# Gate and up by seven block products, and the down product moved between the phases of the next part

## The reference

```python
x = _layer_norm(ALPHA * x + (1 + g1) * mix_out) * ln1_g[l] + ln1_b[l]
h = _layer_norm(x) * (1 + sc2) + sh2
a = silu(einsum('bsd,df->bsf', h, w_gate[l])) * einsum('bsd,df->bsf', h, w_up[l])
ffn = einsum('bsf,fd->bsd', a, w_down[l])
x = _layer_norm(ALPHA * x + (1 + g2) * ffn) * ln2_g[l] + ln2_b[l]
```

## Time and profile before

| | us |
|---|---|
| median of 3 runs | 3360.29 (3359.33 to 3364.14) |
| the profiled execution, its own time | 3362.47 |
| its span, first to last instruction | 3360.4 |
| TensorE busy | 3103.6 |
| VectorE, ScalarE, GpSimd busy | 1487.3, 1029.2, 1120.6 |
| HBM over the span | 90 GB/s |

### The profile page before, as it was taken

One profiled execution on the slowest core, in us unless ns is written; L12 is line 12 of the kernel. 1 busy time (PEld: TensorE's weight loads), 2 busy tenths in 40 slices (PEclk: granted clock), 3 DMA queues, 4 the chain that ended last, 5 costly groups with the idle time before them and its releaser, 6 DMA issues.

```text
span 3360.4 us, 39114 instructions
## 1 busy us (share of the span) xinstructions
PE 3103.6 (92%) x15050; PEld 2592.3 (77%) x15050; DVE 1487.3 (44%) x2194; ACT 1029.2 (31%) x1602; POOL 1120.6 (33%) x649
## 2 busy tenths in 40 slices
PE   8798997899999979997799999979999998999995
PEld 1587886566666646786799999879999987999994
DVE  2343342888888845687221221452112254221225
ACT  1111111777777755123212112221211122112111
POOL 0122231011111125465333333553333364333333
PEclk9899998999999998998899999989999998999997
DMA  9222324321212106354511112131111213111111
GB/s 351 98 72 83 104 81 125 89 63 51 74 57 63 51 23 206 107 176 155 176 63 63 62 62 100 51 125 66 62 66 68 100 51 126 62 62 62 62 63 50
DMA packets 163881, 305.30 MB, mean 91 GB/s; under 512 B 12846, under 2 KB 100015, under 8 KB 161970
## 3 DMA queue, kind: packets, MB, share of 16 engines
q1 hardware_dynamic: 163766, 303.79, 27.3%
HBM read 237.37 MB, written 66.37 MB: 90 GB/s over the span
## 4 chain that ended last, share of the span: by engine, by line
PE 45%; POOL 3%; issue 2%; DVE 1%; DMA 1%; POOLq 1%; ACT 1%; DVEq 0%; SPq 0%; ACTq 0%
PE ffn_gu L1797 10%; PE ffn_gu L1799 10%; PE ffn_gu L1798 10%; PE ffn_dn L1813 5%; PE ffn_dn L1814 5%; PE ffn_dn L1815 5%; POOL ffn_out L1730 1%; POOL ffn_w_lo L1719 1%; POOLq L1725 1%; DMA ffn_h_in<-scr_h_d 1%; POOL ffn_h_lo L1770 0%; DVE ffn_out L1840 0%; POOL ffn_a_lo L1748 0%; POOL ffn_mv L1724 0%; ACT ffn_h_hi L1675 0%
## 5 line engine op out<-in xcount | busy, mean ns | idle before, releaser
L1797 PE MATMUL ffn_gu<-ffn_h_hi,ffn_w_hi 128*128 128x384 f32 x2112 | 707.6, 335 | 30.6 <-DVE ffn_h_lo L1844 26.0
L1799 PE MATMUL ffn_gu<-ffn_h_hi,ffn_w_lo 128*128 128x384 f32 x2112 | 707.2, 335 | 0.0
L1798 PE MATMUL ffn_gu<-ffn_h_lo,ffn_w_hi 128*128 128x384 f32 x2112 | 707.0, 335 | 0.0
L1719 POOL TENSOR_TENSOR ffn_w_lo<-ffn_w_raw,ffn_w_hi 128x2048 fp32r<-128x2048 f32 x99 | 460.9, 4657 | 407.5 <-ACT ffn_w_hi L1667 406.4
L1859 DVE TENSOR_TENSOR ffn_a_raw<-ffn_sil,ffn_gu 128x384 f32<-128x384 f32 x132 | 73.1, 554 | 945.0 <-PE ffn_gu L1799 944.0
L1797 PEld LDWEIGHTS ffn_gu<-ffn_h_hi,ffn_w_hi 128*128 128x128 f32 x2112 | 397.5, 188 | 32.8 <-issue 26.3
L1798 PEld LDWEIGHTS ffn_gu<-ffn_h_lo,ffn_w_hi 128*128 128x128 f32 x2112 | 397.5, 188 | 1.3
L1799 PEld LDWEIGHTS ffn_gu<-ffn_h_hi,ffn_w_lo 128*128 128x128 f32 x2112 | 397.4, 188 | 0.0
L1813 PE MATMUL ffn_dn<-ffn_w_hi,ffn_a_hi 128*128 128x512 f32 x792 | 315.6, 399 | 46.3 <-DVE ffn_total L1869 17.0
L1871 DVE TENSOR_TENSOR ffn_total<-ffn_total,ffn_dn 128x512 f32<-128x512 f32 x360 | 246.0, 687 | 229.8 <-PE ffn_dn L1815 229.8
L943 DVE TENSOR_REDUCE att_peak<-att_sc 128x1 f32<-128x1024 f32 x256 | 312.6, 1221 | 74.7 <-PE att_sc L761 69.9
(11 more groups left out here) (218 smaller groups left out, 4533.6 us busy)
## 6 DMA issues: line engine op xcount, KB each, us to landing
ffn_w_raw<-in_w_gu SPq DMA_DIRECT2D x132, 512.0 KB, 4.5
ffn_w_raw<-in_w_dn SPq DMA_DIRECT2D x66, 512.0 KB, 4.5
mod_wa<-in_w_ada SPq DMA_DIRECT2D x32, 768.0 KB, 6.7
att_q_t<-scr_qs_d SPq DMA_DIRECT2D x128, 128.0 KB, 2.8
proj_x_in<-in_x SPq DMA_DIRECT2D x18, 512.0 KB, 3.9
tail_x_in<-in_x SPq DMA_DIRECT2D x18, 512.0 KB, 3.4
scr_x_d<-tail_w_raw SPq DMA_DIRECT2D x18, 512.0 KB, 5.4
scr_h_d<-tail_direct SPq DMA_DIRECT2D x18, 512.0 KB, 6.1
```

Source lines behind the costliest of these rows:

```text
L1719: nc.gpsimd.tensor_tensor(w_lo[:, i, :], w_raw[:, i, :], w_hi[:, i, :].bitcast(F32), ALU.subtract).then_inc(wlo_done[i], 1)
L1797: nc.tensor.matmul(dst, w_hi[:, i, cols], h_hi[:, k, tokens], start=(k == 0), stop=False)
L1798: nc.tensor.matmul(dst, w_hi[:, i, cols], h_lo[:, k, tokens], start=False, stop=False)
L1799: m = nc.tensor.matmul(dst, w_lo[:, i, cols], h_hi[:, k, tokens], start=False, stop=(k == KD - 1))
```

## The change

Gate and up are each one product of a 1024 x 256 weight block with 1024 x 768 activations, and each of these is cut into 2 x 2 blocks and computed by the Strassen-Winograd scheme: seven block products of 4 steps (half of the width), in place of eight. For this:

- `fourier_and_mix` writes seven operands per pair of tiles to `h7_d` in place of `h2_d`: three blocks of `h2` and four sums of blocks (`operands` on VectorE, behind the tile's own work). `x1_n` is computed by ScalarE with a bias from GpSimd. The 1 of 1 + g is added where the modulation rows are made.
- A part of `ffn` is two phases, gate (`F = 2 * G`) and up (`F + 1`), each with seven weight operands of 128 x 512, three of them sums that VectorE makes (`sums_w`, `last_sum_w`). The raw weights have one buffer for both phases, and operand j of a phase takes the place of operand j of the phase before. ScalarE and GpSimd split each operand.
- VectorE and ScalarE read each product out of one of 4 banks into `sil` or `up`; most products are added to one or two of the four result blocks (`take`).
- The down product of part G-1 stands between the gate and the up phase of part G; the last part's stands behind its own up phase. Down weights have one raw buffer of half a part. The second half of part G-1's is split in the gate phase of part G, the first half of part G's in its up phase.
- A block's input is 21 chunks of 128 x 512, loaded through 4 slots, two of three split by GpSimd and one by VectorE.
- The sample tiles come first (`FFN_ORDER`), so each block has one gate row but for the end of the last. Output tiles are normalised in `total`; in the last block GpSimd does the shift of four tiles.

The core of the diff, with its new functions (added loops and declarations of the same kind are left out):

```diff
@@ fourier_and_mix
+            def operands(t):
+                b11, b21, b12, b22 = h2[:, 0, 0:4, :], h2[:, 0, 4:, :], h2[:, 1, 0:4, :], h2[:, 1, 4:, :]
+                nc.vector.tensor_tensor(t1, b12, b11, ALU.subtract)
+                nc.vector.tensor_tensor(t3, b22, b12, ALU.subtract)
+                dve.drain()
+                nc.vector.tensor_tensor(t2, b22, t1, ALU.subtract)
+                dve.drain()
+                nc.vector.tensor_tensor(t4, b21, t2, ALU.subtract).then_inc(tsum_done, 1)
-                    normalise(1, before, x1_n[:], x1[:, before, :]).then_inc(n2_done, 1)
+                    nc.scalar.activation(x1_n[:], x1[:, (t - 1) % 2, :], ACT.Identity, bias=mv[:, 1, (t - 1) % 2, 5:6],
+                                         scale=mv[:, 1, (t - 1) % 2, 3:4]).then_inc(n2_done, 1)
@@ ffn, SyncE
-                    for i in range(3):
-                        sp.wait_ge(wlo_done[i], G + 1)
-                        weights(0 if is_part(part, PARTS - 1) else part + 1, i)
+            def weights(part, which, F):
+                if begun(F):
+                    sp.wait_ge(wlo_done, OPERANDS * F)
...
+            def down_weights(part, i, G):
+                if i or begun(G):
+                    sp.wait_ge(dnlo_done, 2 * G + i)
...
+                weights(part, 1, F + 1)
+                down_weights(part - 1, 1, G - 1)
...
+                down_weights(part, 0, G)
+                if closes(part):
...
+                    down_weights(part, 1, G)
+                    if not is_last(b, part):
+                        for c in range(CHUNKS7):
+                            hidden(b + 1, c // PAIRS, c % PAIRS)
+                        weights(0, 1, F + 3)
...
+                else:
+                    weights(part + 1, 0, F + 2)
@@ ffn, ScalarE, a step (refill(j) is split_w(F + 2, j) and, in the closing part, split_h(b + 1, j))
+                copy_first(F, sil[:, 0, 0, :])
+                if not is_part(part, 0):
+                    split_down(G - 1, 1)
...
+                for j in (0, 1):
+                    split_w(F + 1, j)
+                silu(G, 1, 1)
+                split_w(F + 1, 2)
+                silu(G, 0, 0)
...
+                copy_first(F + 1, up[:, 0, 0, :])
+                if not is_part(part, 0):
+                    split_down(G, 0)
+                refill(0)
+                if closes(part):
+                    split_down(G, 1)
+                refill(1)
+                split_a(G, 0)
+                refill(2)
+                split_a(G, 1)
+                split_a(G, 2)
+                refill(3)
+                split_a(G, 3)
+                refill(4)
+                refill(5)
+                refill(6)
@@ ffn, GpSimd, a step: split_w(F + 1, 0 to 6), then the same order from refill(0) on
@@ ffn, TensorE
+            def phase(b, part, F):
+                for j in range(OPERANDS):
+                    pe.wait_ge(wlo_done, OPERANDS * F + j + 1)
...
+                    for k in range(4):
+                        cols = slice(k * P, (k + 1) * P)
+                        nc.tensor.matmul(dst, w_hi[:, j, cols], h_hi[:, j, k, :], start=(k == 0), stop=False)
+                        nc.tensor.matmul(dst, w_hi[:, j, cols], h_lo[:, j, k, :], start=False, stop=False)
+                        m = nc.tensor.matmul(dst, w_lo[:, j, cols], h_hi[:, j, k, :], start=False, stop=(k == 3))
+                    m.then_inc(prod_done, 1)
+            def down(G):
+                pe.wait_ge(dnlo_done, 2 * G + 2)
+                for m_ in range(BANKS):
...
+                    if m_ >= 4 or begun(G):
+                        pe.wait_ge(added, BANKS * G + m_ - 3)
...
+            def step(b, part, G):
+                phase(b, part, 2 * G)
+                if not is_part(part, 0):
+                    down(G - 1)
+                phase(b, part, 2 * G + 1)
+                if closes(part):
+                    down(G)
@@ ffn, VectorE
+            def sums_w(F):
+                dve.wait_ge(raw_landed, 32 * (F + 1))
+                nc.vector.tensor_tensor(both[:], raw[:, 1, 0, :], raw[:, 1, 1, :], ALU.add)
+                dve.drain()
+                nc.vector.tensor_tensor(raw[:, 1, 0, :], raw[:, 0, 0, :], raw[:, 1, 0, :], ALU.subtract)
+                nc.vector.tensor_tensor(less[:], both[:], raw[:, 0, 0, :], ALU.subtract).then_inc(wsum_done, 1)
+            def last_sum_w(F):
+                dve.wait_ge(wlo_done, OPERANDS * F + 2)
+                nc.vector.tensor_tensor(less[:], raw[:, 0, 1, :], less[:], ALU.subtract).then_inc(wsum_done, 1)
+            def take(F, j, first, dst):
+                dve.wait_ge(prod_done, OPERANDS * F + j + 1)
+                return nc.vector.tensor_tensor(dst, first, gu[:, j % 4, 0:HALF], ALU.add)
...
+                first_takes(F, sil, in_gate)
+                if opens:
+                    last_sum_w(F + 1)
+                else:
+                    split_down(G - 1, 1)
+                    sums_w(F + 1)
...
+                last_take(F, sil, 4)
...
+                last_take(F, sil, 5)
+                last_take(F, sil, 6)
...
+                if not opens:
+                    last_sum_w(F + 1)
+                    down(b, part - 1 if isinstance(part, int) else part, G - 1)
+                    if not is_last(b, part):
+                        sums_w(F + 2)
+                first_takes(F + 1, up, in_up)
...
+                multiply(G, 0)
...
+                last_take(F + 1, up, 4)
+                multiply(G, 1)
```

More of the change, by code:

```diff
@@ L1497, in _ @@
             combine(1)
-            for t in range(NT + 1):
+            for t in range(NT + 3):
                 slot, before = t % 2, 1 - t % 2
+                if t >= 4 and t % 2 == 0:
+                    operands(t - 4)
                 if t < NT:
@@ L1576, in ffn @@
+        y_stored = [s.sem(f"y_stored{i}") for i in range(TILES)]
         block = ctx.enter_context(nc.Block())
@@ L1581, in parts @@
                 step(b, 0, PARTS * b)
-                with eng.Fori(1, PARTS - 1) as part:
+                step(b, 1, PARTS * b + 1)
+                with eng.Fori(2, PARTS - 1) as part:
                     step(b, part, PARTS * b + part)
@@ L1647, in step @@
[L1647 to L1656 removed]
+                F = 2 * G
+                tail = b - 1 if b else None
@@ new lines, in step @@
+                if is_part(part, 0):
+                    if tail is not None:
+                        down_weights(0, 0, G)
+                        residual(tail, 2)
+                        residual(tail, 3)
+                        finish(tail, 0)
+                        residual(tail, 4)
+                        finish(tail, 1)
+                    weights(1, 0, F + 2)
+                    if tail is not None:
+                        residual(tail, 5)
+                        finish(tail, 2)
+                        finish(tail, 3)
+                    return
@@ new lines, in split_w @@
+            def split_w(F, j):
+                if j == 0:
+                    act.wait_ge(raw_landed, 32 * (F + 1))
+                if j == 1:
+                    act.wait_ge(wsum_done, 2 * F + 1)
+                if j == 6:
+                    act.wait_ge(wsum_done, 2 * F + 2)
+                if begun(F):
+                    act.wait_ge(prod_done, OPERANDS * (F - 1) + j + 1)
+                src = (raw[:, 0, 0, :], less[:], raw[:, 1, 0, :], both[:], raw[:, 0, 1, :], raw[:, 1, 1, :], less[:])[j]
+                nc.scalar.activation(w_hi[:, j, :], src, ACT.Copy).then_inc(whi_done, 1)
@@ new lines, in split_a, with normalise @@
+            def split_a(G, n):
+                i, c = A_ORDER[n]
+                act.wait_ge(mult_done, 4 * G + n + 1)
+                if n == 0 and begun(G):
+                    act.wait_ge(dn_done, BANKS * G)
+                nc.scalar.activation(a_hi[:, i, c, :], sil[:, i, c, :], ACT.Copy).then_inc(ahi_done, 1)
+            def normalise(b, n):
+                N, j = TILES * b + n, DOWN_ORDER[n]
+                act.wait_ge(rstd_done, N + 1)
+                nc.scalar.activation(total[:, j, :], total[:, j, :], ACT.Identity, bias=mv[:, n, 5:6],
+                                     scale=mv[:, n, 3:4]).then_inc(normed, 1)
@@ L1774, in _, with split_w @@
-            parts(pool, step)
-            rstd(NT - TILES)
-            for T in range(NT - TILES, NT):
-                if T + 1 < NT:
-                    rstd(T + 1)
-                scale(T)
+            def split_w(F, j):
+                pool.wait_ge(whi_done, OPERANDS * F + j + 1)
+                src = (raw[:, 0, 0, :], less[:], raw[:, 1, 0, :], both[:], raw[:, 0, 1, :], raw[:, 1, 1, :], less[:])[j]
+                nc.gpsimd.tensor_tensor(w_lo[:, j, :], src, w_hi[:, j, :].bitcast(F32), ALU.subtract).then_inc(wlo_done, 1)
@@ new lines, in shift, with refill @@
+            def shift(n):
+                tile = total[:, DOWN_ORDER[n], :]
+                pool.drain()
```

(55 more changed lines are left out.)

615 lines of the change are left out of this document (349 added, 266 removed).

## The result

The changed kernel takes **3501.7 us** (median of 4 runs, 3500.75 to 3510.19) against 3360.6 (3359.33 to 3364.14): ratio 1.0424, 95% interval 1.0406 to 1.0442. It is 4.2% slower; the prediction said 1.1% slower, with 3440 as the upper end of its range. The profiled span went from 3360.4 to 3499.1, **+138.7 us**, where the sum of the prediction had +37.

What follows compares the result with a forecast made beforehand. TensorE, busy 92%, was taken to bound the kernel. Terms -137 + 100 + 14 + 18 + 30 + 8 + 4 = +37 us on the profiled 3362.5 gave 3399.5, as a median 3397 us; range 3325 to 3440.

Steps and rivals of the forecast that it cites:

- Removed matmuls, -137: Gate and up phases: 168 matmuls a part in place of 192, 4.16 us less in each of 33 parts, -137 us.
- First wait, before the down product: Steady part: TensorE waits 1.6 us (0.5 to 2.3) for the late-loaded second half of the down weights to be split.
- Second wait, inside it: Steady part: the down product's bank 4 waits 2.1 us (0 to 2.5) for the first down add on VectorE.
- Clock, +14: Steady parts: one in three second waits lowers TensorE's clock, 1.5 us per drop, +14 us (0 to 40).
- Boundaries, +15 each: Two block boundaries: late activation splits, adds, residuals, waits and half clock make 44 us against 28.9, +15 each, +30.
- Start +18, end +8: First load to first down product: 39 us against 21.3, +18; end: GpSimd's scale and shift hold VectorE's port, +8.
- Stage before, +4: Before the feed-forward: normalise moves to ScalarE, four VectorE instructions and a store group follow the last hidden tile, +4 us.
- Rival (d): Clock and boundaries cost more: a drop behind each second wait adds 26, ten more per boundary 20; 3443 us, chance 0.17.
- Rival (b): Down weights in time in steady parts: 3324 us with 1.5 a part, 3284 with no wait at all; chance 0.28.

Runs made afterwards that it cites:

- the reordered kernels: Changed kernel with the second down-weight half loaded ahead of the up weights and the last weight sum behind the fourth down add: 3334.8 us, ratio 0.9925.

## Why the prediction was wrong

- *Removed matmuls, -137*: right. 45.51 us a part where nothing waits, 49.67 before.
- *First wait, before the down product*: right in cause and releaser, short in size. 1.6 predicted, 2.4 on average over 27 parts (1.75 to 3.4). GpSimd's last split ends at 7.5 of the gate in each of the 27, as walked. What differs is the landing of the down half: predicted at 13.8, it came between 14.0 and 15.7, 14.5 on average. From issue to landing, in the part shown and in one with a wait of 3.4:
```profile
ffn_dn_raw<-in_w_dn SPq DMA_DIRECT2D x1, 512.0 KB, 5.2
...
ffn_dn_raw<-in_w_dn SPq DMA_DIRECT2D x1, 512.0 KB, 6.7
```
- *Second wait, inside it*: right, 2.1 predicted. It is 1.9 to 2.2 in 12 parts; in the other 15 the slow matmuls behind the first wait filled it down to 0.6 or less.
- *Restarts*: a term that the sum did not have. Each wait costs some 0.27 us beyond its printed idle, as in the part shown, 0.5 a part with two of them and 14 us in 27.
- *Clock, +14*: right, with more drops than the term speaks of. The clock fell in 24 of the 27 parts. In 15 it fell behind the first wait, and the slow matmuls filled the second, which is what the prediction said of them. In 9, one in three as it had put down, it fell behind the second wait; their down products took 20.4 to 20.6 us in place of 18.8 to 19.1, 1.6 more each (1.5 predicted), 15 us in all. That it would be one in three was a guess. Two of the parts in the windows of the changed kernel, the first the only one of block 0 at 1.00:
```profile
1747.52:1797.69 50.17, 46.05 (x240) 42.52 (x241) 28.11 (x41) 14.26 (x26) 24.48 (x19) 1.00 0.18 63
...
1899.51:1950.08 50.57, 47.70 (x240) 43.67 (x241) 28.15 (x41) 14.26 (x26) 24.54 (x19) 0.97 0.18 62
```
  TensorE was busy 1.65 us longer in the second, where the drop stood behind the first wait. Held up by hand, the clock gives back 0.7 us a part, 18 us in all. So the steady part is 4.8 of waits with their restarts and 0.7 of clock, where the prediction had 3.7 and 0.5; the 34 us by which these parts exceed their term are the later landing and the restarts.
- *Boundaries, +15 each*: **the step that failed**, 52 of the 102 us by which the sum was short; the steady parts are 34, the rest 16. Neither alone would have brought the time into the range: without the 52 it is 3450. A boundary's excess is 70 us and not 44, so the term is +41 each. The timeline of TensorE shows the idles of the first boundary:
```profile
2204.30 0.77 PE L2010 MATMUL ffn_dn<-ffn_dn_hi,ffn_a_hi 128*128 128x512 f32 x1 [14.53 <-issue]
...
2205.29 0.63 PE L2012 MATMUL ffn_dn<-ffn_dn_hi,ffn_a_lo 128*128 128x512 f32 x1
2205.72 0.63 PE L2010 MATMUL ffn_dn<-ffn_dn_hi,ffn_a_hi 128*128 128x512 f32 x1
...
2218.50 0.80 PE L2010 MATMUL ffn_dn<-ffn_dn_hi,ffn_a_hi 128*128 128x512 f32 x1 [2.74 <-DVE ffn_total L2115]
...
2284.47 0.66 PE L1990 MATMUL ffn_gu<-ffn_h_hi,ffn_w_hi 128*128 128x384 f32 x1 [12.69 <-DVE ffn_up L2054]
...
2310.25 0.80 PE L2010 MATMUL ffn_dn<-ffn_dn_hi,ffn_a_hi 128*128 128x512 f32 x1 [5.51 <-DVE ffn_dn_lo L2049]
...
2323.18 0.77 PE L2010 MATMUL ffn_dn<-ffn_dn_hi,ffn_a_hi 128*128 128x512 f32 x1 [5.58 <-DVE ffn_total L2113]
```
  The closing down waits 14.5 (11 predicted), the adds in it 4.0 (6), gate and up of the opening part and the next gate 24.8 (18), the first down 11.1 and half clock with restarts the remaining 15.6 (9 for both). It is the last pair that was far off, 26.7 for 9: each of the five idles shown is followed by matmuls at the lower clock (0.77 to 0.80 us for a first one of 512 columns, where it was 0.49 to 0.50 at the upper, and then 0.43 from one start to the next), and each wait had been priced by itself. All of this boundary's idles but the longest, and one of 1 us that ends at GpSimd, end at VectorE, and VectorE has 109.64 us of work in 161 us there, for 74.69 in 128 before. The run without the shifts shows that its amount counts, for a part of the excess; what sets the rest is argued and not shown. The longest, before the closing down, is GpSimd's, as predicted: its third activation split stands behind splits of hidden chunks, for the first of which GpSimd stood idle 7 us, and ends at 29.2 of the up phase (25.8 predicted). This wait stayed at 14.3 to 15.0 in all runs but the one that split the activations first (6.6) and the one that moved the down product (16.6).
```profile
2187.73 2.54 POOL L1887 TENSOR_TENSOR ffn_h_lo<-ffn_io,ffn_h_hi 128x512 fp32r<-128x512 f32 x2 [7.01 <-ACT ffn_h_hi L1776]
...
2201.94 2.26 POOL L1892 TENSOR_TENSOR ffn_a_lo<-ffn_sil,ffn_a_hi 128x384 fp32r<-128x384 f32 x2
```
- *Start +18, end +8*: near (24.8 and 9.6). *Stage before, +4*: 11.7 by the first gate/up load. It came between 1604.5 and 1611.8 us in the eleven profiles of kernels with this change, so some 6 to 14. Of the 11.7, 5.8 lie ahead of the last transposes; the normalise on ScalarE in front of them, a wait of 6.5 for 3.6 before, makes 3 of these. The four operand instructions add 3.2, their stores 2.0 and the landing 0.7. The rows of before and after:
```profile
1589.44 1.97 PE L1279 MATMUL tail_bank<-keep_ident,tail_x_n 128*128 128x128 f32 x8 [3.57 <-DVE tail_x_n L1473]
...
1595.25 1.97 PE L1304 MATMUL tail_bank<-keep_ident,tail_x_n 128*128 128x128 f32 x8 [6.51 <-ACT tail_x_n L1412]
```
- *Rival (d)*, the clock and the boundaries cost more, has the right side, and its 3443 was passed by 59. Only its boundary half came: it added 10 a boundary by guess, and 26 was right. Its clock half, a drop behind each second wait, did not. *Rival (b)*, down weights in time, is what the reordered kernels are: it put 3284 with no wait at all, and 3334.8 came, since the boundaries cost 42 us more than the sum had, and stage, start and end the other 8.

The numbers of the waits came from walking one steady part through its queues, and they held to 1 us on average. The boundaries were sums of single collisions, without a look at how often TensorE would stand and restart at the lower clock, nor at how full VectorE would be there.

## What to carry to other kernels

When a change moves an operand's load into a phase already holding others, ask which load is needed first and put it first in the queue; the same for the last instruction ahead of the adds that free a bank. These two lines were worth 167 us, where the matmuls left out were worth 137. Where a steady loop has slack, write down for the stretches that break it (openings, closings) how much each engine has to do there, and give each further wait its restart and the lower clock behind it, too.

## What the hardware showed that was not expected

- Idles of 1.75 to 3.4 us ahead of a down product, with a second one inside it, were followed by a lower granted clock in 24 parts of 27 (0.97 over most, 1.00 in three). With the first almost alone (1.7 to 3.5 us, the second 0.3 or less) it fell in 10 of 27 steady parts, with the second alone (0.4 to 2.2 us) in none. Matmuls of 512 columns then start 0.43 us apart in place of 0.227.
- The lock between a VectorE instruction with two SBUF inputs and a GpSimd one showed in each of the 27 steady parts: two of the four sums took 1.51 to 1.78 us where the other two took 0.68 to 0.70. This is what the Trainium skill (SBUF — State Buffer, Who interferes with whom) says, and the trace agrees; the bank reads, with one input in SBUF, kept 0.55 as it says too. Leaving out 2.4 us of GpSimd work a tile made the boundaries shorter by about a quarter of it.
- Waits filled with matmuls that are thrown away kept the clock at 1.00 (the mean of nine parts), and a part took 50.3 us in place of 51.0.
